# Norm weight applied at the gather, and each expert's gate, up and down matrices in one transfer

## The chip, the cores and the metric

The kernel runs on one core of one Trainium2 chip. The metric is the device time of the whole program in microseconds, lower is better: the median of several executions. A profile is one further execution, recorded by the hardware profiler.

## What is computed

A two-layer encoder trunk over 256 tokens of width 1024, all in float32. Cut to what matters here:

```
for l in range(2):
    h = rms_norm(x, norm_mix[l])
    x = x + concat[diff_attn, sparse_attn, latent_attn](h @ w_in[l]) @ w_out[l]
    n = rms_norm(x, norm_ffn[l])                  # norm_ffn: the weight that the change moves
    # router: 1 of 4 groups, then 2 of its 8 experts, for each token
    for e in range(32):
        h_e = silu(n[tokens of e] @ w_gate[l, e]) * (n[tokens of e] @ w_up[l, e])
        x[tokens of e] += gate_weight * (h_e @ w_down[l, e])
out = rms_norm(x, norm_final)
```

The weights `w_gate`, `w_up` (1024 x 512 each) and `w_down` (512 x 1024) of one expert are 6.29 MB together. 2 layers x 32 experts make 402.7 MB, and every expert is computed, for at most 32 tokens at a time.

## The kernel before

**Stages.** Each layer has an attention part (projections with `w_in` in six chunks, 16 attention steps, output projection with `w_out` in two halves), then the router, then the expert part: four rounds (`m`) of eight experts (`BODY`). Within a round the tokens are gathered twice, for four experts each (`QUAD`), by TensorE products with a selection matrix `pick`. The engines are programmed by hand, each with its own instruction list; semaphores order them.

**One expert on the engines.** TensorE multiplies the gathered tokens `xg` by gate and up (`gate_up`, L1751), transposes (L1762, L1765), multiplies by down (`down`, L1776), and adds the weighted rows into PSUM sums (`scatter`, L1786). ScalarE copies `gu_ps` out (`products_out`, L821 frees the gate/up place), takes the exponent (L806) and copies `y` (`y_out`, L832 frees the down place). VectorE makes the hidden values (`hidden`). TensorE runs `products(e)` first and `down_of(e - 1)` behind it, except for the last expert of a round, where `down_of` of the one before comes ahead of it.

**Where weights lie and what loads them.** SyncE (SP) issues nearly all transfers, in the order of its program, and waits for a semaphore ahead of an issue where the target is still in use. All of them go through one queue, q1. The gate/up matrices of expert `e` lie side by side in DRAM (`gate_up`, 32768 bytes in each of 128 partitions) and go to one of four places (`gu_place[e % 4]`: three pairs of slots of `ring`, and `late_place` in `arena`). The down matrix (`w_down`, 16384 bytes in each partition) goes to one of three places (`d_place[e % 3]`: slots 7 and 6 of `ring`, and `xb`). `ring` has eight slots of 16384 bytes per partition; `xb` behind it holds `x` and the attention bias. `loads_of(m)` gives the order of the issues of a round: gate/up of `e`, then down of `e - 1`. L563 issues gate/up, L573 down.

**Before the first expert.** `first_experts(l)` (L465 to L504) loads the first four experts while the attention part runs, each into slots as the `w_in` and `w_out` chunks there come free. Three quarters of expert 3's down matrix go to spare places (`spare`); its last quarter is loaded at L573 once expert 0's down matrix has been used. The 128-fold broadcast row of `norm_ffn` (`gain_ffn`) is loaded here too, at L480.

**The norm weight.** VectorE multiplies `x` by `gain_ffn` into `weighted` (`weight`, L1124); ScalarE scales the result by the row's `rms` and reorders it into `rows` (L642, called `copy`); the gathers read `rows`. The copies of a gather out of PSUM into `xg` are two of 128 x 512 (`gathered`, L642).

**The end of layer 0.** SP loads the chunks of `w_in` of layer 1 into the slots as the last experts are done with them, with nine small vectors (`load_small`, L441) behind the second chunk, then the bias and `w_out`.

**The start.** VectorE waits for `consts_in` at the head of its program, TensorE ahead of its second run of warm-up products (L1474).

## Time and profile before

| | us |
|---|---|
| median of 3 runs | 1176.25 (1175.04 to 1177.41) |
| the profiled execution | 1173.85 |
| its recorded span | 1171.9 |

| engine | busy, us | share of the span |
|---|---|---|
| TensorE, products | 930.9 | 79% |
| VectorE | 335.0 | 29% |
| ScalarE | 195.2 | 17% |
| DMA queue q1, 444.54 MB | | 90.3% of 16 engines |

The two expert parts run from about 158 us to 584 us and from about 738 us to the end. "DMA share" in the rows below is the share of a stretch in which the 16 DMA engines were moving packets; a little over 1 is an artefact of the edges. A packet is one contiguous run of bytes of one partition, so that a transfer into 128 partitions has 8 packets on each of the 16 DMA engines; packets "under 512 B" between long transfers are the notices of completion, 16 for each transfer.

### The profile page before, as it was taken

How to read it: one execution, taken by the hardware profiler on the slowest of the kernel's cores; microseconds unless marked ns; L12 is line 12 of the kernel's file. 1: busy time of each engine (PE TensorE's matmuls, PEld its weight loads, DVE VectorE, ACT ScalarE, POOL GpSimd, SP SyncE). 2: the span in 40 equal slices, each digit the busy share in tenths (PEclk: the TensorE clock that was granted, in tenths of full speed). 3: DMA queues.
4: the chain of work that ended last, by engine and by line, in shares of the span. 5: the costliest groups of instructions: out<-in, count | busy, mean ns of one | idle time of the engine just before them, and what ended most of it. 6: DMA issues, size and time to landing. Idle time of an engine off the chain costs nothing.

```text
span 1171.9 us, 23254 instructions
## 1 busy us (share of the span) xinstructions
PE 930.9 (79%) x10294; PEld 582.0 (50%) x10299; DVE 335.0 (29%) x978; ACT 195.2 (17%) x527; POOL 18.7 (2%) x38
## 2 busy tenths in 40 slices
PE   8999999767567766775899999997776677557765
PEld 5876666434334433543478766664343434234433
DVE  3656552211111111111137465521111111111112
ACT  2234321001000100110112442211010001001002
POOL 1000000000000000000010001000000000000000
PEclk9999999989888888888999999999887888788878
DMA  7956499999999999999998256999999999999995
GB/s 308 404 237 258 200 379 423 435 428 428 427 433 426 429 426 435 425 429 427 401 386 322 80 218 270 382 429 430 427 430 427 429 426 431 428 430 427 428 424 245
DMA packets 34455, 446.16 MB, mean 381 GB/s; under 512 B 9648, under 2 KB 11056, under 8 KB 14256
## 3 DMA queue, kind: packets, MB, share of 16 engines
q1 hardware_dynamic: 33792, 444.54, 90.3%
q8 instruction: 84, 1.38, 0.5%
q10 hardware_dynamic: 560, 0.09, 0.0%
q14 instruction: 19, 0.16, 0.0%
HBM read 443.57 MB, written 1.05 MB: 379 GB/s over the span
## 4 chain that ended last, share of the span: by engine, by line
DMA 50%; PE 45%; issue 2%; DVE 1%; ACT 1%; another core or an unknown queue 0%; SPq 0%; ACTq 0%; POOLq 0%; POOL 0%; DVEq 0%
DMA ring<-in_w_down 18%; DMA arena<-in_gate_up 14%; DMA xb<-in_w_down 14%; PE pv L1751 10%; PE pj L1374 8%; PE tr L1776 5%; DMA ring<-in_gate_up 3%; PE pj L1380 2%; PE tr L1735 2%; PE pj L1486 2%; PE pj L1786 2%; PE pj L1606 2%; PE pj L1581 1%; PE pj L1615 1%; PE lg L1404 1%
## 5 line engine op out<-in xcount | busy, mean ns | idle before, releaser
L1751 PE MATMUL pv<-ring,xT 128*32 128x256 f32 x3072 | 228.5, 458 | 110.8 <-DMA ring<-in_gate_up 110.8
L1751 PEld LDWEIGHTS pv<-ring,xT 128*32 128x32 f32 x3072 | 110.2, 127 | 218.0 <-DMA ring<-in_gate_up 109.8
L1222 DVE TENSOR_SCALAR arena<-arena 128x128 f32<-128x128 f32 x64 | 14.5, 227 | 667.2 <-ACT arena L806 666.9
L1751 PE MATMUL pv<-arena,xT 128*32 128x256 f32 x1024 | 85.5, 500 | 67.1 <-DMA arena<-in_gate_up 67.1
L642 ACT ACTIVATE arena<-pv 128x256 f32<-128x256 f32 x64 | 24.6, 384 | 513.3 <-PE pv L1751 513.3
L1374 PE MATMUL pj<-xT,ring 128*128 128x256 f32 x448 | 100.2, 381 | 0.0
L1776 PE MATMUL tr<-ring,arena 128*32 128x256 f32 x1360 | 81.9, 380 | 16.5 <-issue 10.1
L1751 PEld LDWEIGHTS pv<-arena,xT 128*32 128x32 f32 x1024 | 38.7, 139 | 112.6 <-DMA arena<-in_gate_up 73.4
L1374 PEld LDWEIGHTS pj<-xT,ring 128*128 128x128 f32 x448 | 84.3, 190 | 12.9 <-issue 1.1
L1786 PE MATMUL pj<-arena 32*128 32x256 f32 x512 | 72.5, 400 | 6.7 <-ACT arena L642 6.7
L1786 PE MATMUL lg<-arena 32*128 32x256 f32 x512 | 72.5, 401 | 0.0
L1776 PEld LDWEIGHTS tr<-ring,arena 128*32 128x32 f32 x1360 | 44.1, 109 | 48.6 <-issue 14.3
L642 ACT ACTIVATE arena<-tr 128x256 f32<-128x256 f32 (+3 forms) x106 | 41.2, 407 | 156.9 <-PE tr L1776 134.7
L1735 PE MATMUL tr<-arena,rows 128*128 128x128 f32 x448 | 58.6, 293 | 7.5 <-issue 7.5
L1735 PEld LDWEIGHTS tr<-arena,rows 128*128 128x128 f32 x448 | 55.7, 206 | 12.4 <-issue 12.4
L1223 DVE RECIPROCAL arena<-arena 128x128 f32<-128x128 f32 x64 | 61.0, 953 | 2.2
L1786 PEld LDWEIGHTS pj<-arena 32*128 32x128 f32 x512 | 44.5, 184 | 23.1 <-issue 22.0
L1776 PE MATMUL tr<-xb,arena 128*32 128x256 f32 x640 | 38.4, 380 | 8.5 <-DMA xb<-in_w_down 4.7
L1786 PEld LDWEIGHTS lg<-arena 32*128 32x128 f32 x512 | 43.8, 184 | 0.0
L1765 PE MATMUL pv<-con,arena 128*32 128x128 f32 x1024 | 41.2, 279 | 0.0
L1762 PE MATMUL pv<-con,arena 128*128 128x128 f32 x128 | 32.4, 335 | 9.5 <-ACT arena L642 9.5
L1762 PEld LDWEIGHTS pv<-con,arena 128*128 128x128 f32 x128 | 20.2, 207 | 37.3 <-issue 19.7
(237 smaller groups left out, 856.8 us busy)
## 6 DMA issues: line engine op xcount, KB each, us to landing
ring<-in_gate_up SPq DMA_DIRECT2D x42, 4096.0 KB, 48.5
ring<-in_w_down SPq DMA_DIRECT2D x38, 2048.0 KB, 41.4
arena<-in_gate_up SPq DMA_DIRECT2D x14, 4096.0 KB, 41.9
xb<-in_w_down SPq DMA_DIRECT2D x18, 2048.0 KB, 40.8
ring<-in_w_in_chunks SPq DMA_DIRECT2D x10, 2048.0 KB, 21.3
ring<-in_gate_up SPq DMA_DIRECT2D x10, 2048.0 KB, 8.2
ring<-in_w_out_halves SPq DMA_DIRECT2D x4, 2048.0 KB, 33.2
arena<-in_gate_up SPq DMA_DIRECT2D x4, 2048.0 KB, 49.4
```

Of the source, the lines that this page charges most:

```text
L642: return nc.scalar.activation(out, in_, ACT.Copy, **k)
L1223: own.link(v.reciprocal(e_neg, e_neg))
L1374: ins = mm(out, w[:, j], xT[:, j, :], start=(j == 0), stop=(j == KD - 1))
L1380: ins = mm(out, src[:, j, t * P:(t + 1) * P], weights(i, n)[:, j, c:c + m], start=(j == 0), stop=(j == KD - 1))
L1486: ins = mm(bank[:, 0:R5], xT_raw[:, j, t * P:(t + 1) * P], weights(0, n5)[:, j, :], start=(j == 0), stop=(j == KD - 1))
L1606: mm(pj[:, half], mixT_up[:, t, k - KD // 2, :], chunk(6 + half, 512)[:, k, :], start=(k == KD // 2), stop=False)
L1735: ins = mm(wide_ps[:, j * n:(j + 1) * n], rows[:, t, j * P:(j + 1) * P], pick[:, t, 0:n], start=(t == 0), stop=(t == TOK - 1))
L1751: ins = mm(gu_ps[i * CAP:(i + 1) * CAP, :], xg[:, j, c:c + CAP], w, start=(j == 0), stop=(j == KD - 1), tile_position=(0, i * CAP), skip_g ...
L1762: turn_(h_ps[:, c].rearrange("p h s -> p (h s)"), by_step[:, c], ident)
L1765: ins = mm(pgt_ps[k * CAP:(k + 1) * CAP, t * P:(t + 1) * P], pgate[:, t, i, :], ident, start=True, stop=True, tile_position=(0, k * CAP), ...
L1776: ins = mm(tr[i * CAP:(i + 1) * CAP, 0, 0:SEQ], hid[:, b, k % 2, k // 2, :], rows_of[k][:, SEQ * i:SEQ * (i + 1)], start=(k == 0), stop=(k ...
L1786: ins = mm(sums[i][:, SEQ * t:SEQ * (t + 1)], pgT[r, b, t, :], y[r, :], start=False, stop=last, tile_position=(i * CAP, 0), skip_group_che ...
```

## The change

**Layout.** In DRAM one array `experts` holds gate, up and down of an expert side by side, 49152 bytes in each partition. In SBUF `ring` and `xb` become one tensor `ring_xb`; its first nine slots are three places of three slots each (`whole`). A place takes all of one expert. `late_place` is a fourth place, for the gate/up matrices of expert 3 and of expert 31 (`LATE`, `LAST`); the down matrices of those two go to four spare pieces. Experts 4 to 30 go round the three places.

**Transfers.** Expert 0, and experts 6 to 28, come in one transfer each, which waits for the place's gate/up and down to be both used. Expert 1, 2, 4, 5, 29, 30 still come in parts. The down matrix of expert 31 comes in four pieces instead of three.

**Norm weight.** `gain_ffn`, its transfer and the VectorE products are gone. ScalarE copies `x` with the scale `rms` into `rows`, and each gather is copied to `xg` in eight pieces of 128 x 128, each with the weight of its 128 columns as scale (`gain_G`, one value per partition); TensorE waits piece by piece.

**Waits.** `consts_in` is waited for later, at the first use of the identity. `load_small` of layer 1 stands behind the third chunk of `w_in` and waits for expert 31's down matrix to be used, since one of its targets is a spare piece.

```diff
+PLACES, LATE = 3, 3
+AHEAD = PLACES + 1
+LAST = N_EXPERTS - 1
+def place(e):
+    return e if e < AHEAD else LATE if e == LAST else (e - AHEAD) % PLACES
 def loads_of(m):
-    order = [("gu", 0)]
-    for e in range(1, BODY - 1):
-        order += [("gu", e), ("d", e - 1)]
-    late = [("gu", BODY - 1), ("d", BODY - 2)] if m == ROUNDS - 1 else [("d", BODY - 2), ("gu", BODY - 1)]
-    return [(kind, m * BODY + e) for kind, e in order + late + [("d", BODY - 1)]]
+    first, last = max(m * BODY, AHEAD), (m + 1) * BODY
+    if m == 0:
+        order = [("d", AHEAD), ("gu", AHEAD + 1), ("d", AHEAD + 1)]
+        return order + [("all", e) for e in range(AHEAD + 2, last)]
+    if m < ROUNDS - 1:
+        return [("all", e) for e in range(first, last)]
+    order = [("gu", LAST - 2), ("gu", LAST - 1), ("d", LAST - 2), ("gu", LAST), ("d", LAST - 1), ("d", LAST)]
+    return [("all", e) for e in range(first, LAST - 2)] + order
...
+        whole = [ring_xb[:, 3 * i * SLOT:3 * (i + 1) * SLOT] for i in range(PLACES)]
+        gu_place = [flat.rearrange("p (j n) -> p j n", j=KD) for flat in [w[:, 0:2 * SLOT] for w in whole] + [late_place]]
+        d_place = [w[:, 2 * SLOT:].rearrange("p (k n) -> p k n", k=KE) for w in whole]
...
                 sp.wait_ge(win_used[1], l + 1)
-                sp.dma_start(gu_place[0], gu[0]).then_inc(gu_full[0], 16)
                 sp.wait_ge(win_used[2], l + 1)
+                sp.dma_start(whole[0], experts_d[l * N_EXPERTS]).then_inc(gu_full[0], 16)
...
-                sp.dma_start(gain_ffn, bcast_row(norm_ffn, l, D_MODEL)).then_inc(gain_f_in, 16)
+                sp.dma_start(spare[3], down[LATE][:, 3]).then_inc(spare_full[3], 16)
...
+                        i, n = place(e), l * N_EXPERTS + e
+                        if kind != "d":
+                            sp.wait_ge(gu_used[i], at(l, FILLS[i], uses(i, e)))
+                        if kind != "gu":
+                            sp.wait_ge(d_used[i], at(l, FILLS[i], uses(i, e)))
+                        if kind == "all":
+                            sp.dma_start(whole[i], experts_d[n]).then_inc(gu_full[i], 16)
...
-                    act.wait_ge(x_weighted, at(l, TOK, t + 1))
+                    act.wait_ge(x_added, at(l, PARTS, (2, PARTS)[t]))
...
-                        for half in range(2):
-                            act.wait_ge(wide_done, at(r, WIDE, gather_use(q) + half))
-                            copy(xg[:, 4 * half:4 * half + 4, :].rearrange("p j s -> p (j s)"), tr[:, half]).then_inc(wide_read, 1)
+                        for j in range(KD):
+                            if j % 4 == 0:
+                                act.wait_ge(wide_done, at(r, WIDE, gather_use(q) + j // 4))
+                            copy(xg[:, j, :], wide_ps[:, j * P:(j + 1) * P], scale=gain_G[:, l, j:j + 1]).then_inc(wide_read, 1)
...
-                weight(0, 0, D_MODEL).then_inc(x_weighted, 1)
...
-                own.mark(weight(1, 512, D_MODEL))
...
-                weight(1, 0, 512).then_inc(x_weighted, 1)
```

On SyncE's queue, in the first round of layer 0, behind the load of the rest of expert 4's gate/up: `in_gate_up` 128x8192 is gate and up of an expert, `in_w_down` 128x4096 its down matrix, `in_experts` 128x12288 all three. The waits name the semaphores of the places (`gu_used`, `d_used`). Before:

```order
L503 DMA ring<-in_gate_up 128x4096 [waits gu_used0]
L573 DMA ring<-in_w_down 128x1024 [waits d_used0]
L563 DMA ring<-in_gate_up 128x8192 [waits gu_used1]
L573 DMA ring<-in_w_down 128x4096 [waits d_used1]
L563 DMA ring<-in_gate_up 128x8192 [waits gu_used2]
L573 DMA xb<-in_w_down 128x4096 [waits d_used2]
L573 DMA ring<-in_w_down 128x4096 [waits d_used0]
L563 DMA arena<-in_gate_up 128x8192 [waits gu_used3]
```

And now:

```order
L504 DMA ring_xb<-in_experts 128x4096 [waits gu_used0]
L577 DMA ring_xb<-in_experts 128x4096 [waits d_used0]
L572 DMA ring_xb<-in_experts 128x8192 [waits gu_used1]
L577 DMA ring_xb<-in_experts 128x4096 [waits d_used1]
L567 DMA ring_xb<-in_experts 128x12288 [waits d_used2,gu_used2]
L567 DMA ring_xb<-in_experts 128x12288 [waits d_used0,gu_used0]
```

The quarter of expert 3's down matrix (128x1024) has left this place, and from expert 6 on one issue with two waits stands for two issues with one each; the load of expert 7 now waits for the place of expert 4 rather than for that of expert 3.

On SyncE's queue at the end of layer 0, from the last gate/up matrix to the first small vector of layer 1. Before:

```order
L561 DMA arena<-in_gate_up 128x4096
L573 DMA ring<-in_w_down 128x4096 [waits d_used0]
L570 DMA ring<-in_w_down 128x2048 [waits d_used1]
L570 DMA ring<-in_w_down 128x1024 x2
L517 DMA ring<-in_w_in_chunks 128x3520 [waits gu_used0]
L517 DMA ring<-in_w_in_chunks 128x4096 [waits gu_used0]
L441 DMA lowrank<-in_mla_q_norm 128x256
```

And now:

```order
L570 DMA arena<-in_experts 128x4096
L577 DMA ring_xb<-in_experts 128x4096 [waits d_used2]
L575 DMA xT<-in_experts 128x1024 [waits d_used3]
L575 DMA arena<-in_experts 128x1024
L575 DMA lowrank<-in_experts 128x1024
L575 DMA arena<-in_experts 128x1024
L520 DMA ring_xb<-in_w_in_chunks 128x3520 [waits gu_used0]
L520 DMA ring_xb<-in_w_in_chunks 128x4096 [waits gu_used0]
L520 DMA ring_xb<-in_w_in_chunks 128x4096 [waits d_used0]
L443 DMA lowrank<-in_mla_q_norm 128x256 [waits d_used3]
```

The third chunk of `w_in` now stands ahead of the small vectors, and these wait for `d_used3`, the use of expert 31's down matrix.

## Rows read from the trace of the kernel before

**Rows 1.** windows of the trace (busy time of each engine, PEclk, DMA share, GB/s)

```profile
60.00:132.00 72.00, 71.54 (x354) 47.59 (x353) 40.99 (x116) 29.00 (x99) 1.02 (x1) 1.00 0.53 205
132.00:160.00 28.00, 27.54 (x182) 20.87 (x185) 17.25 (x68) 11.64 (x22) 3.34 (x3) 1.00 0.92 374
...
250.00:540.00 290.00, 199.10 (x2696) 116.71 (x2696) 45.92 (x115) 26.66 (x70) 0.00 (x0) 0.85 1.00 429
830.00:1130.00 300.00, 208.31 (x2826) 121.32 (x2826) 46.37 (x117) 27.61 (x73) 0.00 (x0) 0.84 1.00 428
```

**Rows 2.** the chain of waits in order of time

```profile
252.86 41.62 DMA xb<-in_w_down
```

**Rows 3.** the transfer of the norm weight (first and last start, us)

```profile
L480 SPq DMA_DIRECT2D arena<-in_norm_ffn x2: 431/431/431, 102.9 to 682.9; - x2
```

**Rows 4.** DMA queues, 250 to 350 us (packets, MB, share of 16 engines)

```profile
DMA packets 1975, 42.87 MB, mean 429 GB/s; under 512 B 215, under 2 KB 215, under 8 KB 215
...
q1 hardware_dynamic: 1968, 42.76, 99.9%
```

**Rows 5.** the same, 33 to 40 us

```profile
q1 hardware_dynamic: 203, 2.98, 99.5%
```

**Rows 6.** the same, 558 to 565 us

```profile
q1 hardware_dynamic: 205, 2.98, 100.5%
```

**Rows 7.** timeline of TensorE, one expert of round 2, layer 0

```profile
304.48 5.80 PE L1751 MATMUL pv<-ring,xT 128*32 128x256 f32 x64 [5.93 <-DMA ring<-in_gate_up]
310.11 1.90 PE L1776 MATMUL tr<-ring,arena 128*32 128x256 f32 x32
```

**Rows 8.** timeline of SyncE's queue, the same stretch

```profile
312.12 0.33 SPq L573 DMA_DIRECT2D ring<-in_w_down  x1
```

**Rows 9.** line L482, a transfer of 2048 KB with nothing ahead of it

```profile
DMA to landing us min/median/max: 7.3/7.4/7.4
```

**Rows 10.** chain of waits, round 4 of layer 1

```profile
1036.61 6.67 PE pv L1751 x63
...
1062.05 4.31 PE pv L1751 x63
```

**Rows 11.** line L503, the last part of expert 4's gate/up

```profile
DMA to landing us min/median/max: 9.9/10.3/10.7
```

**Rows 12.** timeline of SyncE's queue, after expert 4

```profile
203.14 0.33 SPq L573 DMA_DIRECT2D ring<-in_w_down  x1
```

**Rows 13.** timeline of all engines, 0 to 20 us

```profile
6.07 1.29 DVE L911 TENSOR_TENSOR rows<-arena,gain_T 128x512 f32<-128x512 f32 x2 [5.15 <-remote]
6.82 9.13 PE L1486 MATMUL pj<-ring,rows 128*128 128x440 f32 x24
...
15.00 0.35 DVE L915 TENSOR_SCALAR arena<-con,rms 128x128 f32<-128x128 f32 x1 [0.90 <-POOL rms L606]
...
15.78 0.61 PE L1469 MATMUL lg<-arena,con 128*128 128x128 f32 x4
```

**Rows 14.** timeline, 128 to 175 us: rms of the last token tile and the router

```profile
151.48 0.84 POOL L606 TENSOR_TENSOR rms<-ssq,con 128x1 f32<-128x1 f32 x1 [13.84 <-DVE ssq L1129]
...
152.38 0.26 DVE L1137 SCALAR_TENSOR_TENSOR arena<-pv,rms,br 128x40 f32<-128x40 f32 x1 [0.47 <-POOL rms L606]
```

**Rows 15.** a copy of 128x128 by ScalarE

```profile
204.11 0.28 ACT L806 ACTIVATE arena<-pv 128x128 f32<-128x128 f32 x1 [0.54 <-PE pv L1765]
```

**Rows 16.** timeline of TensorE, the end of layer 0

```profile
576.72 1.93 PE L1776 MATMUL tr<-ring,arena 128*32 128x256 f32 x32 [1.21 <-DMA ring<-in_w_down]
...
581.76 0.16 PEld L1776 LDWEIGHTS tr<-ring,arena 128*32 128x32 f32 x8 [0.33 <-DMA ring<-in_w_down]
```

**Rows 17.** timeline of SyncE's queue, the start of layer 1

```profile
588.45 1.88 SPq L517 DMA_DIRECT2D ring<-in_w_in_chunks  x4
```

**Rows 18.** timeline of VectorE, the start of layer 1

```profile
602.71 1.41 DVE L949 SCALAR_TENSOR_TENSOR arena<-arena,rms,lowrank 128x256 f32<-128x256 f32 x4 [0.42 <-POOL rms L606]
...
611.88 0.35 DVE L976 SCALAR_TENSOR_TENSOR arena<-arena,xb 128x128 f32<-128x128 f32 x1 [6.91 <-ACT arena L733]
```

More of the change, by code:

```diff
@@ L169, in upto @@
     def upto(last):
-        return sum(D_LOADS.get(n, 1) for n in range(last) if n < N_EXPERTS - 1 and n % D_PLACES == e % D_PLACES)
+        return sum(D_LOADS.get(n, 0) for n in range(last) if place(n) == place(e))
     return 16 * at(layer, upto(N_EXPERTS), upto(e + 1))
@@ L575, in _ @@
-            sp.wait_ge(gu_used[GU_PLACES - 1], DEPTH * GU_FILLS)
+                        i, n = place(e), l * N_EXPERTS + e
[5 more added lines that the diff above has]
+                            sp.dma_start(whole[i], experts_d[n]).then_inc(gu_full[i], 16)
+                        elif kind == "gu" and e == LAST:
+                            for part, (a, b) in enumerate(LAST_STEPS):
+                                sp.dma_start(gu_place[i][:, a:b], gu_v[n][:, a:b]).then_inc(last_steps_in[part], 16)
+                        elif kind == "gu":
+                            sp.dma_start(gu_place[i], gu_v[n]).then_inc(gu_full[i], 16)
+                        elif e == LAST:
+                            for k in range(KE):
+                                sp.dma_start(spare[k], down_v[n][:, k]).then_inc(last_in[k], 16)
+                        else:
+                            sp.dma_start(d_place[i], down_v[n]).then_inc(d_full[i], 16)
@@ L1771, in down @@
                     for k in range(KE):
[L1772 to L1774 removed]
+                        if in_pieces:
+                            pe.wait_ge(last_in[k], 16 * (l + 1))
                         for i in range(4):
```

215 lines of the change are left out of this document (95 added, 120 removed).

## Prediction

> **What bounds the kernel now.** I read the page's slices first, then the windows by stage, then the DMA queues, and the engines' timelines last. The page gives TensorE 79% busy and q1 90.3%, and both are averages over two kinds of stage. The windows separate them [rows 1]. From 60 to 132 us TensorE is busy 71.5 of 72 us and the DMA share is 0.53: the attention part hangs on TensorE, and transfers have room. From 250 to 540 us, and from 830 to 1130 us in layer 1, TensorE is busy only 199.1 of 290 and 208.3 of 300 us, at a granted clock of 0.85, while the DMA share is 1.00 at 428 to 429 GB/s. From 132 to 160 us the share is already 0.92. So each expert part is one stream of bytes that starts near 132 us of its layer and is full from about 160 us on; its end comes at (bytes of the stream) / (rate), whatever the other engines do, as long as each load is issued in time. One expert is 6.29 MB, 14.66 us at 429 GB/s. The chain of waits names SyncE's waits for places too (a load 41.62 us between issue and landing [rows 2]), but 41.6 us is nearly three experts of queue: such a wait is no loss while the queue is full. I therefore price the change by what it takes out of the stream, what it makes each byte cost, what it moves at the stream's start, and whether a load can now be late.
>
> **Bytes taken out.** The broadcast row of the norm weight (0.52 MB) is loaded at 102.9 and 682.9 us, in the stretch with room [rows 1, 3]. Its transfer goes, and the last quarter of expert 3's down matrix, 0.52 MB, takes its place there; that quarter leaves the full stream. 0.524 / 429 = 1.22 us for each layer, **-2.44 us** in all. This is sure as far as the stream is full, which rows 1 say.
>
> **Fewer and longer packets.** A transfer of 16384-byte rows, alone in the queue, shows what a packet costs: from 33 to 40 us q1 moves 2.98 MB (182 packets of 16384 bytes) in 99.5% of 16 x 7 us, 612 ns each [rows 5]; from 558 to 565 us the same 2.98 MB in 100.5%, 618 ns each [rows 6]. From 250 to 350 us q1 moves 42.76 MB in 1968 packets, of which 215 are notices; the other 1753 are 16384 or 32768 bytes, and the bytes say 896 and 857 of them [rows 4]. They take 99.9% of 1600 us, so a 32768-byte packet takes (1598.4 - 896 x 612) / 857 = 1225 ns, or 1219 ns by the other value. Twice 612 less 1225 is -1 ns, twice 618 less 1219 is 17 ns: a packet costs between nothing and 17 ns beyond its bytes. I take the middle, 9 ns, since nothing singles out an end. A whole expert saves 8 packets and one notice on each engine, 9 x 9 = 81 ns. Of the whole experts 6 to 28 lie in the full stream, 23 for each layer (expert 0 has room): 46 x 0.081 = **-3.7 us**, with ends at 0 and 46 x 9 x 17 ns = -7.0 us. Expert 31's down matrix has one piece more and 8 rows more for each engine, +0.08 us at each layer's end, **+0.2**.
>
> The Trainium skill ("DMA: Bandwidth & Descriptors", section "Anatomy of one DMA") gives a DMA about 2.0 us of fixed cost beside its bytes. By that alone, 46 transfers fewer would be worth 92 us. The trace speaks against it here: a stream with two transfers in each 14.66 us runs at a DMA share of 1.00 [rows 1], so the fixed part of one lies beside the bytes of another. The same page puts the ceiling at 435 GB/s ("Where 436 GB/s comes from"); an estimate by that page is that no packet size could give more than 1.4% of the stream.
>
> **Can a load be late?** Before, up to three experts were queued; now the load for expert e + 3 waits until both parts of expert e are used. In the trace the first product of an expert starts at 304.48, its 32 products and the down product of the expert before it end near 312, and SyncE issues at 312.12: 7.6 us after the landing [rows 7, 8]. A transfer of 2.10 MB with nothing ahead lands 7.4 us after its issue [rows 9], 2.5 us more than its bytes take. The next load is thus ready 10.1 us after a landing where 14.66 are allowed: 4.5 us to spare. The worst place is the fourth round, where TensorE reads the overflow count: products that follow expert 23's at 1036.61 start at 1062.05, 25.4 us later [rows 10]. Expert 25 would land 29.3 us after expert 23, the products of 24 end at 25.4 + 4.3 = 29.7, so only half a us is lost there and the margin stays above 2. In steady state I book nothing.
>
> The one tight place is at the stream's start, where TensorE still runs ahead. The rest of expert 4's gate/up is issued at 162.0 and lands 10.3 us later, at 172.3 [rows 11]. Behind it now come expert 4's down, all of 5 and all of 6: 14.68 MB, 34.2 us, so expert 6 lands near 206.5. Expert 7 must go to expert 4's place, whose down matrix is used at 203.14 [rows 12]; issued then, it lands at 203.14 + 2.5 + 14.66 = 220.3, against 221.2 for an unbroken stream. A margin of 0.9 us; TensorE's extra waits in the gathers can eat it. I book **+0.3 us** for each layer, ends 0 and 1.5, **+0.6** in all.
>
> **The norm weight.** VectorE loses three multiplies. The one on the way to the last gather stands while GpSimd takes 0.84 us for the rms, and the router's first step idles 0.47 us until that rms is there [rows 14]; TensorE's last router product ends at about the same moment, so I book 0, at best -0.3 for each layer. ScalarE's copies become eight of 128 columns. One such copy takes 0.28 us [rows 15], a little more with a scale; a gate/up step (one eighth of 3.8 to 5.8 us [rows 7]) lasts 0.47 us or more, so the copies stay ahead of TensorE. 0; if that cover were gone, 8 x 0.28 - 1.2 = 1.0 us at the two gathers of a first round, the others lie in TensorE's idle time.
>
> **The start.** VectorE's first multiply starts at 6.07 us after the wait for `consts_in`, TensorE's first product 0.75 us later [rows 13]. Without that wait the product can start about 0.5 us earlier; the next gate is VectorE's second diagonal, ready at 15.35, against TensorE at 15.78 [rows 13]: **-0.4 us**, which shifts everything behind it. Ends 0 and -0.5.
>
> **Between the layers.** The small vectors now wait for expert 31's down product, near 582 us [rows 16]. Ahead of them in the queue are three chunks, 5.9 MB or 13.7 us after the last expert, so they land near 600 us. VectorE needs them at 602.71, and after them it idles 6.91 us before 611.88 [rows 18]: 9 us of cover, 0. The third chunk was issued at 588.45 with three others [rows 17]; it is earlier now, the others within a few us.
>
> **Sum.** -2.4 - 3.7 + 0.2 + 0.6 - 0.4 = -5.7 us. The profiled execution takes 1173.85 us (span 1171.9 and 2 us around it), so 1168.1 by the sum; the median of the runs is 2.4 us above it, 1176.25 - 5.7 = **1170.5**.
>
> **Rivals.** (1) The rows are cut again, or a packet's time is all bytes: the packet term is 0 and the time 1174.2, within 0.2%. For it: the lower end of the estimate from rows 4 to 6 is zero. Against it: 16384- and 32768-byte rows both show as one packet each, and the two windows' mean is above zero. 0.14. (2) Late loads make it slower. The place: the issue behind `y_out`. The mechanism is that it must come within 14.66 - 2.5 = 12.2 us of a landing, against 7.6 now. If the queue needs more than one transfer of lead, because some of the 16 engines run ahead, each us missed costs 1 us on every transfer; confined to the 14 experts behind a gather at 1 us each it gives +14 - 5.7, 1184.5; on all 46, 1216. It decides where the lead falls below 2.5 us plus the engines' spread. Against it: margins of 4.5 and above 2 us. 0.07. (3) The same late issue only at the stream's start, at its full 1.5 us in each layer: +2.4, 1172.9, inside the forecast's range. (4) The fixed-cost rule: faster by tens of us, 1084; at a DMA share of 1.00 there is nothing to win it from. 0.01.
>
> **How the numbers follow.** The forecast with its unknowns (packets 0 to -7.0, start of the stream 0 to 3, rms 0 to -0.6) spans about 1166 to 1174 and has 0.78. Below it lies little; above it, rival 1 at 1174.2 belongs in the range and rival 2 does not. Range **1166.0 to 1174.8**. Faster than 1173.9 (0.2% is 2.35 us, about what a measurement of this kernel can tell from no change): 0.77 + 0.01 and a part of rival 1's spread, 0.80. Same: 0.13. Slower: 0.07.
>
> **What would show it.** The DMA share in the stretch of whole experts stays at 1.00 and the rate rises from 429 to 431 or 432 GB/s; packets of 49152 bytes take less than one of each kind before. If the rate stays at 429, the packet term was wrong; if the share falls below 1, loads are late, and the idle time stands behind `y_out` on SyncE. TensorE's first product starts near 6.3 us, layer 0's last down product 3.5 us earlier than now. What would make it wrong: a lower rate for the 49152-byte pitch, or a gap around expert 7 of more than 1.5 us.

## The result and the profile after the change

| | before | after |
|---|---|---|
| median of the runs | 1175.04 us (1174.32 to 1177.41) | 1168.97 us (1167.60 to 1169.34) |
| profiled execution, span | 1171.9 us | 1166.2 us |
| ratio after / before, 95% interval | | 0.9945, 0.9932 to 0.9958 |

The change makes the kernel 6.1 us faster between the medians; the interval goes from 4.9 to 8.0 us. The forecast was 5.7 us faster, 1170.5 us in a range of 1166.0 to 1174.8. (It counted from 1176.25, the median of three runs; over five runs the kernel before has 1175.04.) A second set of five runs of the changed kernel gave 1169.05 us beside 1174.65.

The windows of the changed kernel (busy time of each engine, granted clock, DMA share, GB/s) answer to [rows 1]:

```profile
60.00:132.00 72.00, 71.53 (x353) 47.37 (x352) 40.83 (x116) 29.02 (x99) 1.02 (x1) 1.00 0.52 205
132.00:160.00 28.00, 27.26 (x182) 20.72 (x184) 14.55 (x63) 12.55 (x28) 2.12 (x3) 1.00 0.93 375
...
250.00:540.00 290.00, 200.92 (x2760) 117.61 (x2760) 44.48 (x112) 32.36 (x100) 0.00 (x0) 0.85 1.00 429
830.00:1130.00 300.00, 209.08 (x2890) 122.45 (x2890) 47.90 (x120) 33.42 (x103) 0.00 (x0) 0.85 1.00 429
```

They look like those of before, and that is what the reader has to see first: the expert parts are still one full stream, and the rate that a window prints (whole GB/s) is too coarse for a change of half a percent. The prediction's own sign ("If the rate stays at 429, the packet term was wrong"), read from these lines, would have struck out a term that was right. A finer ruler is needed. The products of an expert start when its load has landed, so in a stretch where TensorE waits for every expert their starts are the landings of the stream. The timeline of TensorE in layer 0 of the changed kernel (start, duration, and in brackets the idle time and what ended it):

```profile
282.09 5.65 PE L1746 MATMUL pv<-ring_xb,xT 128*32 128x256 f32 x64 [4.90 <-DMA ring_xb<-in_experts]
296.63 3.89 PE L1746 MATMUL pv<-ring_xb,xT 128*32 128x256 f32 x64 [1.31 <-DMA ring_xb<-in_experts]
311.17 6.43 PE L1746 MATMUL pv<-ring_xb,xT 128*32 128x256 f32 x64 [6.84 <-DMA ring_xb<-in_experts]
```

Twice 14.54 us. The kernel before, whose products at 304.48 stand in [rows 7], has the next ones at

```profile
319.10 5.41 PE L1751 MATMUL pv<-ring,xT 128*32 128x256 f32 x64 [5.01 <-DMA ring<-in_gate_up]
```

so 14.62 us. Some steps of both kernels are longer (15.0 us, say), but these are the quiet ones, and they are 0.08 us apart. In bytes that is 6.29 MB in 14.62 us and in 14.54 us, 430.3 and 432.7 GB/s: the rate did rise, as the prediction said.

The end of layer 0 in the changed kernel, TensorE again: the second half of expert 31's gate/up, expert 30's down product, and the last quarter of expert 31's.

```profile
567.80 2.02 PE L1746 MATMUL pv<-arena,xT 128*32 128x256 f32 x32 [2.05 <-DMA arena<-in_experts]
572.75 3.59 PE L1770 MATMUL tr<-ring_xb,arena 128*32 128x256 f32 x32 [1.25 <-DMA ring_xb<-in_experts]
...
579.43 0.61 PE L1770 MATMUL tr<-arena 128*32 128x256 f32 x8
```

Before, the same three stood at 571.82, 576.72 and 581.76 ([rows 16] has the last two; 581.76 is the weight load that opens the last quarter). The stream arrives 4.0 us earlier, the layer ends only 2.4 us earlier (layer 1's first product starts at 584.61, before at 586.98). Between them stands expert 30's down product: 3.59 us for 32 products that took 1.93 us before [rows 16]. The window of 570 to 575 us says why, PEclk is 0.77:

```profile
570.00:575.00 5.00, 3.33 (x42) 1.80 (x46) 2.09 (x5) 0.64 (x2) 0.00 (x0) 0.77 1.04 426
```

For part of that window TensorE ran at the lower of its two levels (1.2 instead of 2.4 GHz), after idle times of 2.05 and 1.25 us between short pieces of work. No term of the forecast spoke of that. In layer 1 the same product took 1.93 us in this execution.

### The profile page after: what moved, and what is told of

It is laid out like the page before. It is cut to its first block, busy times and chain, and to the rows that moved or that the text cites. A ratio compares the mean times of both kernels' runs of the same rounds, so it can differ in the third digit from the quotient of the medians.

```text
span 1166.2 us, 23346 instructions
## 1 busy us (share of the span) xinstructions
PE 920.8 (79%) x10299; PEld 578.4 (50%) x10299; DVE 329.8 (28%) x972; ACT 212.6 (18%) x623; POOL 16.3 (1%) x38
## 4 chain that ended last, share of the span: by engine, by line
DMA 49%; PE 47%; issue 1%; DVE 1%; ACT 1%; POOL 0%; ACTq 0%; POOLq 0%; SPq 0%; DVEq 0%
DMA ring_xb<-in_experts 49%; PE pv L1746 13%; PE pj L1371 8%; PE tr L1770 6%; PE pj L1377 2%; PE pj L1481 2%; PE pj L1601 2%; PE pj L1780 2%; PE pj L1576 1%; PE pj L1610 1%; PE lg L1401 1%; PE pv L1760 1%; PE tr L1411 1%; PE tr L1677 1%; PE tr L1730 1%
## 5 line engine op out<-in xcount | busy, mean ns | idle before, releaser
L1746 PE MATMUL pv<-ring_xb,xT 128*32 128x256 f32 x3840 | 286.2, 459 | 181.7 <-DMA ring_xb<-in_experts 181.7
L1746 PEld LDWEIGHTS pv<-ring_xb,xT 128*32 128x32 f32 x3840 | 135.7, 127 | 320.7 <-DMA ring_xb<-in_experts 197.5
L1770 PE MATMUL tr<-ring_xb,arena 128*32 128x256 f32 x1920 | 116.7, 383 | 19.8 <-issue 15.2
L1371 PE MATMUL pj<-xT,ring_xb 128*128 128x256 f32 x448 | 100.2, 381 | 0.0
L1770 PEld LDWEIGHTS tr<-ring_xb,arena 128*32 128x32 f32 x1920 | 64.2, 110 | 63.7 <-issue 21.6
L1371 PEld LDWEIGHTS pj<-xT,ring_xb 128*128 128x128 f32 x448 | 84.1, 190 | 13.1 <-issue 1.1
L646 ACT ACTIVATE xT<-tr,gains 128x128 f32<-128x128 f32 x128 | 36.4, 370 | 66.8 <-PE tr L1730 66.7
L646 ACT ACTIVATE arena<-pj 64x256 f32<-64x256 f32 (+2 forms) x48 | 21.0, 442 | 71.0 <-PE pj L1371 52.4
L699 ACT ACTIVATE arena<-arena,nmax 128x128 f32<-128x128 f32 (+1 forms) x64 | 28.6, 447 | 25.2 <-DVE nmax L1046 24.8
```

Of the source, the lines that this page charges most:

```text
L646: return nc.scalar.activation(out, in_, ACT.Copy, **k)
L699: ins = nc.scalar.activation(prob[:, s % 2, m * nk(t):(m + 1) * nk(t)], logit[:, s % 2, m * nk(t):(m + 1) * nk(t)], ACT.Exp, bias=nmax[:, ...
L1371: ins = mm(out, w[:, j], xT[:, j, :], start=(j == 0), stop=(j == KD - 1))
L1746: ins = mm(gu_ps[i * CAP:(i + 1) * CAP, :], xg[:, j, c:c + CAP], w, start=(j == 0), stop=(j == KD - 1), tile_position=(0, i * CAP), skip_g ...
L1770: ins = mm(tr[i * CAP:(i + 1) * CAP, 0, 0:SEQ], hid[:, b, k % 2, k // 2, :], rows_of[k][:, SEQ * i:SEQ * (i + 1)], start=(k == 0), stop=(k ...
```

## The experiments

All kernels but the first are the changed kernel as it is or with one edit (two edits where the name has two parts), timed against the kernel before (1174.4 to 1175.0 us, by the set). Two more, with delayed loads, follow at the end of this section. The table has, beside the time, three numbers from the timelines: when the second half of expert 31's gate/up starts (the end of the stream as TensorE sees it), and what expert 30's down product took, in layer 0 and layer 1.

| kernel | median us | ratio (95%) | expert 31, layer 0 / 1 | down 30, us |
|---|---|---|---|---|
| before | 1174.7 | 1 | 571.82 / 1151.12 | 1.93 / 1.94 |
| changed, first | 1168.97 | 0.9945 (0.9932 to 0.9958) | 567.80 / 1145.35 | 3.59 / 1.93 |
| changed, again | 1169.05 | 0.9953 (0.9940 to 0.9966) | 567.81 / 1145.82 | 3.31 / 1.93 |
| two pieces | 1170.38 | 0.9965 (0.9952 to 0.9978) | 569.78 / 1147.62 | 1.93 / 1.93 |
| six pieces | 1183.92 | 1.0085 (1.0072 to 1.0098) | 576.64 / 1160.61 | 1.93 / 1.93 |
| quarter in the stream | 1170.58 | 0.9969 (0.9959 to 0.9980) | 568.60 / 1144.86 | 1.93 / 1.93 |
| expert 7 in two | 1168.24 | 0.9949 (0.9936 to 0.9963) | 567.58 / 1145.09 | 3.48 / 3.39 |
| first wait back | 1168.55 | 0.9958 (0.9944 to 0.9971) | 567.94 / 1143.21 | 1.93 / 3.62 |
| zeros at the end | 1167.36 | 0.9942 (0.9929 to 0.9956) | 568.09 / 1143.23 | 1.93 / 1.93 |
| zeros and expert 7 in two | 1167.21 | 0.9936 (0.9922 to 0.9949) | 568.22 / 1144.55 | 1.93 / 1.93 |
| two pieces, zeros | 1170.59 | 0.9960 (0.9945 to 0.9974) | 569.78 / 1147.21 | 1.93 / 1.93 |
| quarter, zeros | 1169.78 | 0.9951 (0.9935 to 0.9966) | 570.10 / 1147.30 | 1.93 / 1.93 |

An interval is about 1.5 us to each side, so two rows of the table that are 1 us apart are not told apart by their times. Rows of different sets carry the drift of the kernel before too, up to 0.6 us. The columns from the timelines are of one profiled execution each. In two places, the quarter with zeros in layer 0 and the zeros in layer 1, the product follows right behind the products of zeros, so the landing was a little earlier than the number.

One more number from the same executions ties the columns to the time. From the start of expert 31's second half in layer 1 to the end of the profiled execution it is 22.7 to 22.8 us in nine of the twelve rows, six pieces and the kernel before among them. It is 24.2 and 24.3 us in the two whose down product of layer 1 took 3.39 and 3.62 us. In the quarter's, 24.75 us, the last piece of expert 31's down matrix landed late:

```profile
1156.31 0.64 PE L1770 MATMUL tr<-arena 128*32 128x256 f32 x8 [1.37 <-DMA arena<-in_experts]
```

So the time is the end of the stream, and the clock or a late last piece on top of it.

**The changed kernel again.**

> The changed kernel once more, beside the experiments of the same call. Both theories: 5 to 7 us under the kernel before (the first measurement gave 6.1 between the medians), 1168 to 1170 us. It is the base line for the three kernels that follow.

1169.05 us, as expected. Expert 31 started at 567.81 us in layer 0, and expert 30's down product ran at the lower clock there too (3.31 us).

**The price of a packet.** Each of the 46 whole loads as two transfers, then as six:

```
-  sp.dma_start(whole[i], experts_d[n]).then_inc(gu_full[i], 16)
+  sp.dma_start(gu_place[i], gu_v[n]).then_inc(gu_full[i], 16)
+  sp.dma_start(d_place[i], down_v[n]).then_inc(gu_full[i], 16)
```

> The changed kernel with each of the 46 whole loads issued as two transfers again, rows of 32768 and of 16384 bytes, to the same places, behind the same waits, and used only when both have landed. Nothing moves but the number of packets. Theory (a packet costs some 9 ns beside its bytes, and a transfer one notice on each of the 16 engines): 8 packets and one notice more for each engine and expert, 81 ns, so 3.7 us slower than the changed kernel, about 1172. Rival (the packets cost nothing, and the gain is in the bytes, the start or the order of the first loads): no difference, 1168 to 1169.

> The same with six transfers of 8192 byte rows for each of the 46 loads, so that the price of a packet shows several times over. Theory: 40 packets and 5 notices more for each engine and expert at 9 ns, 0.405 us, times 46 = 18.6 us slower than the changed kernel, about 1187; at the upper end of the estimate from the trace of before, 17 ns, 33 us. Rival (a packet's time is its bytes alone): no difference. The DMA share stays at 1.00 in both; the rate tells them apart, 417 GB/s against 430.

Two pieces: 1170.38 us, 1.3 us above the changed kernel, between theory and rival. Six pieces: 1183.92 us, 14.9 us above, where 18.6 and 0 were the bets; the rival is dead. The quiet steps on TensorE's timeline say it without the scatter of whole runs. Two pieces, then six pieces:

```profile
297.40 3.83 PE L1748 MATMUL pv<-ring_xb,xT 128*32 128x256 f32 x64 [1.16 <-DMA ring_xb<-in_experts]
312.01 6.57 PE L1748 MATMUL pv<-ring_xb,xT 128*32 128x256 f32 x64 [6.97 <-DMA ring_xb<-in_experts]
```

```profile
284.63 5.25 PE L1750 MATMUL pv<-ring_xb,xT 128*32 128x256 f32 x64 [5.22 <-DMA ring_xb<-in_experts]
299.53 3.83 PE L1750 MATMUL pv<-ring_xb,xT 128*32 128x256 f32 x64 [2.07 <-DMA ring_xb<-in_experts]
314.42 5.69 PE L1750 MATMUL pv<-ring_xb,xT 128*32 128x256 f32 x64 [7.25 <-DMA ring_xb<-in_experts]
```

14.61 us in two pieces, 14.90 and 14.89 in six, 14.54 in one. Against one piece, two have 9 packets and notices more on each engine, six have 45 more: 0.07 / 9 = 7.8 ns and 0.355 / 45 = 7.9 ns. One price fits both.

The steps alone can't say that it is the packet that costs: in both kernels a transfer more is nine packets and notices more, and 71 ns for each transfer fits them as well. The kept traces do, since they have every packet's own time. In the full stream the medians are 312 ns for 8192 bytes, 612 for 16384, 1214 for 32768, 1815 for 49152 and 9 for a notice. Each 16384 bytes more are 601 to 602 ns, so every packet has about 11 ns beside its bytes, whatever its size. The packets' times add up to 1.01 of the window in six pieces and to 1.00 in one, so they overlap a little, and 7.9 ns is what the stream pays.

The queue of the six pieces from 250 to 350 us shows the same without TensorE:

```profile
q1 hardware_dynamic: 5747, 41.88, 100.8%
```

41.88 MB where the changed kernel moved 43.11 MB in 985 packets in the same 100 us. A window of 100 us cuts rows of 49152 bytes at its ends, so this one is only good for the sign.

**Why two pieces cost only 1.3 us.** Their stream ended 2.0 us later in layer 0 (569.78 against 567.80), but their down product ran at the full clock and the changed kernel's did not. So the same two kernels were compared with the clock held up, by products of zeros in waits that are there anyway:

```
   if in_pieces and j == first:
+      if n == 1:
+          keep_warm(5)
       pe.wait_ge(last_steps_in[n], 16 * (l + 1))
...
   turned(BODY - 1)
+  keep_warm(4)
   down_of(BODY - 2)
```

> The changed kernel with nine products of zeros added at the end of each layer: five between the halves of expert 31's gate/up, four ahead of expert 30's down product, all in time in which TensorE waits for a transfer (gaps of 1.2 to 2.05 us, a product of zeros takes 0.23). They add zeros to a sum. Theory: at the end of layer 0 the granted clock falls to the lower level (0.77 from 570 to 575 us), expert 30's down product takes 3.59 us there where it takes 1.93 in layer 1 and took 1.93 before, and this keeps 1.66 us of the gain: with the engine busy it takes 1.93, and the whole is 1.5 us faster than the changed kernel, about 1167.4. Rival (that product is hidden behind expert 31's down matrix, which lands at 578.7): no difference, or slower by what the zeros take.

> The 46 whole loads in two transfers each, as in the earlier run, and the nine products of zeros in the waits at a layer's end, as in the other. That run was only 1.3 us slower than the changed kernel, but its last expert came 2.0 us (layer 0) and 2.3 us (layer 1) later, and its down product there ran at the full clock where the changed kernel's ran at the lower one. Theory (the lower clock hid the price of the packets): with the clock held up in both, the two pieces cost 46 x 0.073 us = 3.4 us against the kernel with the zeros alone (1167.4), 1170 to 1171. Rival (the packets are worth 1.3 us and the rest is scatter): 1168.7.

The zeros alone: 1167.36 us, 1.6 us under the changed kernel's 1169.0, as bet. The end of layer 0:

```profile
571.72 1.04 PE L1716 MATMUL pj<-zeros 128*128 128x512 bf16 x4
572.98 1.93 PE L1772 MATMUL tr<-ring_xb,arena 128*32 128x256 f32 x32 [0.22 <-DMA ring_xb<-in_experts]
...
578.10 0.64 PE L1772 MATMUL tr<-arena 128*32 128x256 f32 x8
```

Expert 30's down matrix landed 0.2 us later than in the changed kernel (572.98 against 572.75), its product took 1.93 us and the layer's last product starts 1.3 us earlier (578.10 against 579.43). The same window has PEclk 1.00:

```profile
570.00:575.00 5.00, 4.11 (x58) 1.94 (x54) 2.10 (x5) 0.66 (x2) 0.00 (x0) 1.00 1.02 419
```

Two pieces with the zeros: 1170.59 us, 3.2 us above the zeros alone, with 3.4 expected. The two were timed in different sets; beside their own kernels of before the difference is 2.8 us. No run of one is as fast as the slowest of the other (1169.77 and up against 1168.42 and down). The packets are worth about 3.3 us of this kernel by the quiet steps, and the lower clock hid about half of it in the first comparison. Of the seven profiled executions in the table with the new order and without the zeros, four had this product at the lower clock in one layer or in both; of the four with the zeros, none. The times show a gain of the zeros of 1.6 us for the changed kernel, and 0.8 and -0.2 us for the quarter and the two pieces, whose down products were at the full clock in their profiled execution without them. A single one of these differences is at the edge of the scatter. The timelines are plainer: layer 1's first product starts at 584.2 to 584.6 us in the three kernels whose down product of layer 0 was slow, and at 583.2 to 583.5 us in the three (first wait back, and the two with zeros) where it was not and the stream was the same.

**The bytes.** Expert 3's last quarter goes back behind expert 3's gate/up, and its new place stays empty:

```
-  sp.wait_ge(lg_done, at(l, NS, 8))
-  sp.dma_start(spare[3], down[LATE][:, 3]).then_inc(spare_full[3], 16)
...
   sp.dma_start(gu_place[LATE], gu[LATE]).then_inc(gu_full[LATE], 16)
+  sp.wait_ge(lg_done, at(l, NS, 8))
+  sp.dma_start(spare[3], down[LATE][:, 3]).then_inc(spare_full[3], 16)
```

> The changed kernel with the last quarter of expert 3's down matrix (0.52 MB) loaded behind expert 3's gate/up again, in the full stream, where it stood before, and nothing in its new place. This takes back what the norm weight's row made room for. Theory: 1.22 us for each layer at 429 GB/s, 2.4 us slower than the changed kernel, about 1171; the landing of every later load comes 1.2 us later. Rival (the stream's start has idle time that takes it up, since loads there wait for places): under 1 us.

> The quarter of expert 3's down matrix in the full stream, as in the earlier run, and the nine products of zeros. Theory (expert 7's load is set by TensorE's use of expert 4, so of the 1.22 us in each layer only about half is gained): 1.2 us slower than the kernel with the zeros alone, about 1168.6. Rival (the bytes count in full, 2.44 us, and the earlier 1.5 us had the clock's scatter in it): 1169.8.

1.5 us slower without the zeros, 2.4 us with them (2.0 beside their own kernels of before). That is nearer to the full 2.44 us than to the 1.2 of the second run's theory, but with intervals of 1.5 us neither is ruled out.

The edit is not quite the kernel before: here the quarter is loaded from 144 to 146 us, where it was issued at 168.99 before, behind the last part of expert 4's gate/up. That place was dearer than its bytes. The last part of expert 4's gate/up, issued at 161.98, landed 10.7 us later (the longest of [rows 11]), at 172.7. The quarter behind it (line L573, issued at 168.99):

```profile
DMA to landing us min/median/max: 7.1/7.1/7.1
```

It landed at 176.1, 3.4 us after the load ahead of it, where its bytes take 1.22 us; in layer 1 it was 3.25 us by the landings kept in the trace. Its 128 packets of 4096 bytes took 280 ns each on average, 281 in layer 1, where such packets take 159 ns at the layers' other places, such as 109 to 118 us, and 162 to 164 at the layers' ends. (Only the program's first transfer has 237.) On each engine that is 8 x 0.12 = 1.0 us above the price of the bytes, in each layer. In the changed kernel the quarter is loaded ahead of the full stream, where its packets take 159 ns, and in these two runs they take 170 to 178 ns. No run put the quarter back at its old place, and why its packets were slow there is not known.

What the start of the stream shows is small: with the quarter behind expert 3's gate/up, the products of experts 6 and 7 start at

```profile
209.42 5.32 PE L1746 MATMUL pv<-ring_xb,xT 128*32 128x256 f32 x64 [3.56 <-DMA ring_xb<-in_experts]
223.95 3.83 PE L1746 MATMUL pv<-ring_xb,xT 128*32 128x256 f32 x64 [2.19 <-DMA ring_xb<-in_experts]
```

a quiet step of 14.53 us. In the changed kernel they are 14.94 us apart, and there the load of expert 7 comes a little late:

```profile
207.62 5.37 PE L1746 MATMUL pv<-ring_xb,xT 128*32 128x256 f32 x64 [2.44 <-DMA ring_xb<-in_experts]
222.56 3.84 PE L1746 MATMUL pv<-ring_xb,xT 128*32 128x256 f32 x64 [2.55 <-DMA ring_xb<-in_experts]
```

**The late load of expert 7.** Its gate/up is issued behind the products of expert 4, its down matrix behind expert 4's down product:

```
-  return order + [("all", e) for e in range(AHEAD + 2, last)]
+  order += [("all", AHEAD + 2), ("gu", AHEAD + 3), ("d", AHEAD + 3)]
+  return order + [("all", e) for e in range(AHEAD + 4, last)]
```

> The changed kernel with expert 7's load issued as gate/up (behind the products of expert 4 alone) and down (behind expert 4's down product), so that the queue has work while TensorE finishes expert 4. In the changed kernel the DMA share is 0.94 from 205 to 210 us of layer 0, where it was 1.04 before. Theory (the late load of expert 7 costs the slowest engine 0.4 us in each layer: expert 7 lands 14.94 us after expert 6, a quiet expert 14.53): the whole is 0.5 to 0.8 us faster than the changed kernel, less 0.15 for one packet more in each row; the share there is 1.0 again. Rival (the slowest of the 16 engines still has work when the load comes late, so only the others idle): the share returns to 1.0 and the time stays, within 0.2 us.

> The changed kernel with both small changes: products of zeros in TensorE's waits at the end of a layer, and expert 7's load in two. Theory: the first is worth 1.2 to 1.7 us (a down product at the lower clock in one of the two layers), the second nothing that can be measured (0.3 us by the first try, while the slowest engine had work left), so 1167 to 1168 us, at least as fast as any so far. Rival (they add up): 1166.5.

The window of 205 to 210 us, in the changed kernel and then with the load in two:

```profile
205.00:210.00 5.00, 2.56 (x28) 1.16 (x28) 1.62 (x4) 0.00 (x0) 0.00 (x0) 0.75 0.94 364
```

```profile
205.00:210.00 5.00, 2.73 (x32) 1.18 (x28) 1.67 (x4) 0.00 (x0) 0.00 (x0) 0.75 0.99 423
```

The hole in the share closes. The time hardly answers: 1168.24 against 1169.0 without the zeros, 1167.21 against 1167.36 with them, both inside the scatter. The timelines say why. Expert 7's products start anywhere from 222.56 to 224.07 us in the four profiled executions that have the same loads up to there (changed first and again, first wait back, zeros), but expert 12's start at 296.63 to 296.91 in all four, and at 296.30 and 296.79 with the load in two. What the late load costs at expert 7 is made up by expert 12, within 0.3 us. That is the rival of the first run (only the faster engines idle), and the second run's bet (nothing that can be measured) held.

**The start.** TensorE waits for the constants ahead of its first product again:

```
+  if l == 0:
+      pe.wait_ge(consts_in, 16)
   def turn_in(t):
```

> The changed kernel with TensorE's wait for the constants put back ahead of its first product. Theory of the prediction: 0.4 us slower, TensorE's first product at 6.8 us and not at 6.47. What the two traces suggest instead: the first product comes 0.35 us later, and the first expert's products start at 158.0 us all the same, as they do in both kernels (157.98 and 158.02), so no difference in the time.

1168.55 us, no difference. The profiled execution did not show the later first product either: it is at 6.53 us with the wait back, and at 6.24 to 6.79 us in the twelve profiled executions of the new order without it. So the 0.35 us between the two first traces is no larger than what executions of one program differ by, and this run can't test it. What the traces do show is where such a gain would end. TensorE's first product in the changed kernel, and the first products of expert 0:

```profile
6.47 9.02 PE L1481 MATMUL pj<-ring_xb,rows 128*128 128x440 f32 x24
...
158.02 3.83 PE L1746 MATMUL pv<-ring_xb,xT 128*32 128x256 f32 x64
```

Before, they stood at 6.82 [rows 13] and 157.98. TensorE is 0.30 us ahead up to its products at 147.81 us (148.11 before); then VectorE adds their result at

```profile
150.28 0.42 DVE L1127 TENSOR_TENSOR ring_xb<-tr,ring_xb 128x256 f32<-128x256 f32 x1 [2.01 <-PE tr L1631]
```

which is 0.50 us behind the end of those products; before it was 0.15 us. All thirteen profiled executions of the new order have this 0.50 us, whatever their start, and their first expert starts at 157.89 to 158.72 us. Why VectorE starts that much later is open.

**How much lead a load has.** GpSimd delays each whole load by four or by ten small operations (the code is shortened):

```
   rms_of(own, base, 7, 15, 16)
+  for n, e in enumerate(WHOLE):
+      pool.wait_ge(d_used[place(e)], at(l, FILLS[place(e)], uses(place(e), e)))
+      for _ in range(4):                                   # 10 in the second
+          own.link(tensor_tensor(idle, idle, con[C_HALF], ALU.pow))
+      pool.sem_inc(delayed, 1)
...
+  sp.wait_ge(delayed, at(l, len(WHOLE), WHOLE.index(e) + 1))
   sp.dma_start(whole[i], experts_d[n]).then_inc(gu_full[i], 16)
```

> The changed kernel with a delay ahead of each of the 46 whole loads: GpSimd waits for the place, does four small linked operations of about 0.6 us each (2.5 us), and only then lets SyncE issue. Theory (4.5 us of lead to spare in the steady state): the margin takes it up, time as the changed kernel, 1168 to 1170, although faster engines may run dry, so that the mean DMA share falls below 1.00. Rival (the lead has to cover the spread of the 16 engines too, 4 to 5 us between the first and the last of a transfer): 2.5 + 4.5 - 4.5 = 2.5 us late for every second load, some 50 us slower.

> The delay ahead of each of the 46 whole loads made longer: ten linked operations of GpSimd and not four, 6 us where it was 2.4. The short delay cost 11.9 us over the changed kernel, so the margin is used up at about 2.4 us in places and not yet everywhere. Theory (a load must be issued 12.2 us after the landing of the one before it, it is issued 7.6 after; what is late beyond that is lost once for every two loads): 6 - 4.6 = 1.4 us over two loads, 32 us, and with the 0.5 us for each load that the short delay cost beside it, 30 to 45 us slower than the changed kernel, 1200 to 1213. Rival (all of the added 3.6 us is lost on every load, since the lead is gone already): 1180.5 + 46 x 3.6 = 1346; half of that, if it is lost once for every two loads: 1263.

The short delay: 1180.51 us (ratio 1.0050, 1.0034 to 1.0066), 11.5 us slower than the changed kernel, neither nothing nor 50. The long one: 1229.18 us (1.0469, 1.0444 to 1.0494), 60 us slower, beyond the 30 to 45 of the theory and far from 178. The timeline of the long delay in round 2 of layer 0 (GpSimd's rows are the delay itself, SyncE issues 0.15 us behind their end; the products start when their load has landed):

```profile
290.77 5.50 PE L1757 MATMUL pv<-ring_xb,xT 128*32 128x256 f32 x64 [8.25 <-DMA ring_xb<-in_experts]
298.16 6.26 POOL L641 TENSOR_TENSOR idle<-idle,con 128x1 f32<-128x1 f32 x10 [11.30 <-ACTq L849]
305.55 3.83 PE L1757 MATMUL pv<-ring_xb,xT 128*32 128x256 f32 x64 [1.71 <-DMA ring_xb<-in_experts]
...
322.55 6.62 PE L1757 MATMUL pv<-ring_xb,xT 128*32 128x256 f32 x64 [9.36 <-DMA ring_xb<-in_experts]
...
331.05 6.27 POOL L641 TENSOR_TENSOR idle<-idle,con 128x1 f32<-128x1 f32 x10 [13.51 <-ACTq L849]
...
356.36 5.15 PE L1757 MATMUL pv<-ring_xb,xT 128*32 128x256 f32 x64 [5.52 <-DMA ring_xb<-in_experts]
```

Counted from the end of the delay, the load issued at 304.4 lands at 322.55, 18.1 us later and 17.0 us after the one before it; the load issued at 337.3 lands at 356.36, 19.0 us later. Its bytes take 14.54 us, so a whole load needs a lead of 3.6 to 4.5 us, not 2.5, and has to be issued within 10.0 to 10.9 us of a landing. The changed kernel issues about 7.6 us after it, as before [rows 7, 8]: a margin of 2.4 to 3.3 us. The changed kernel itself has one load at this limit: expert 7's, issued at 203.2 when 4.4 us were left to the landing before it, lands 19.3 us later and 0.4 us late. The short delay sits just at the same edge:

```profile
284.24 6.48 PE L1757 MATMUL pv<-ring_xb,xT 128*32 128x256 f32 x64 [6.21 <-DMA ring_xb<-in_experts]
292.60 2.50 POOL L641 TENSOR_TENSOR idle<-idle,con 128x1 f32<-128x1 f32 x4 [14.00 <-ACTq L849]
299.59 3.83 PE L1757 MATMUL pv<-ring_xb,xT 128*32 128x256 f32 x64 [1.29 <-DMA ring_xb<-in_experts]
...
314.12 5.27 PE L1757 MATMUL pv<-ring_xb,xT 128*32 128x256 f32 x64 [6.88 <-DMA ring_xb<-in_experts]
```

Issued at 295.1, 10.9 us after the landing at 284.24, this load still lands a quiet 14.53 us behind its forerunner, while others of this run come 0.8 to 2 us late. The rival's claim that the spread of the engines needs lead of its own was half right: the lead is 1 to 2 us longer than a lone transfer says, not 4.5.

The Trainium skill gives about 2.0 us of fixed cost for a transfer ("DMA: Bandwidth & Descriptors", section "Anatomy of one DMA") and puts most of it into the confirmation that the last byte has landed. The section is on transfers that GpSimd issues; these are issued by SyncE, so it bears on them, and on the prediction's fourth rival, only as a rough guide. Here the runs show that a fixed part is lead and not time of the stream: six pieces have 230 transfers more than one and cost 14.9 us, 65 ns each, where 2.0 us each would be 460 us.

## Why the prediction was right, point by point

- **The bound** was read rightly: in both kernels and the variants of the table the time follows the end of the stream, to 0.1 us where the clock stays up and the last piece is not late.
- **Packets: -3.7 us booked, 3.2 measured** (two pieces against one, clock held up), 3.3 by the quiet steps (46 x 0.071). Of the range of 0 to 17 ns the prediction took the middle, 9 ns, and said that nothing singled it out; it measured 7.9 ns. That it came so near is luck in part, the sign and the mechanism are not. The range of 0 to 17 ns came from windows whose edges cut packets; the starts of products gave the number in two lines, and could have been read from the kernel before for its own step.
- **Bytes: -2.44 us booked, 2.4 and 1.5 measured** by the two pairs, for a quarter that stands earlier than before. At its old place it took about 1.0 us more in each layer than its bytes, by its packets' times: some 4.4 us in all. The step that was off is "0.524 / 429 = 1.22 us for each layer", which took the rate of long packets for a transfer of 4096-byte ones without looking at its landing.
- **Late load at the stream's start: +0.6 us booked** for both layers, nothing found. The place was right, and the step from expert 6 to 7 is 0.4 us too long in layer 0 (up to 2.3 in the other executions), but by expert 12 it is made up within 0.3 us, and closing the hole gave 0.15 to 0.8 us, which the times can't tell from nothing. The prediction took a late landing at one expert for a loss of the stream.
- **Steady state: nothing booked, nothing lost**, but with less to spare than written, 2.4 to 3.3 us and not 4.5. The step that was off is the lead, taken as 2.5 us from a transfer alone in the queue [rows 9]; it is 3.6 to 4.5 us.
- **Norm weight: nothing**, as booked. ScalarE's eight copies end in time (expert 0's products start 0.04 us later than before), and VectorE's first router step starts at 152.43 us, 152.38 before [rows 14], although three multiplies are gone. No run moved the norm weight by itself, so this rests on the timelines.
- **The start: -0.4 us booked, nothing found.** The step that failed is "which shifts everything behind it". The first expert is not earlier: VectorE's 0.35 us more at 150 us would take up such a gain. Whether the first product is earlier at all is not shown, since executions differ by as much. The prediction had followed the gain to 15.78 us and not to the end of the attention part.
- **Between the layers: nothing**, as booked: VectorE takes the small vectors at 600.35 us, 15.7 us after TensorE's first product of layer 1 at 584.61, and before at 602.71 [rows 18], 15.7 us after 586.98.
- **The end of a layer: missed.** The prediction said that layer 0's last down product would come 3.5 us earlier. The stream came 4.0 us earlier and TensorE gave back 1.66 us, because expert 30's down product ran at the lower clock. It happened in one of two layers in this execution, and in 5 of the 14 layers of the seven without zeros. The sum has no term for it.
- **The stream gave more than booked:** 4.0 us in layer 0 and 3.4 in layer 1 (5.77 less the 2.37 by which layer 1 starts earlier; 2.6 to 4.2 in the other executions with whole loads), 7.4 against 5.5 us. Two pieces with the zeros, which has the packet sizes of before for these loads, is 4.1 to 4.3 us faster than the kernel before (3.1 to 6.5 by the interval), of which the bytes at 429 GB/s explain 2.4. The timelines place the other 1.7 to 1.9 us ahead of expert 12 in each layer. From expert 12 to 28 the two kernels take the same time, first before, then two pieces with the zeros:

```profile
289.72 3.90 PE L1751 MATMUL pv<-ring,xT 128*32 128x256 f32 x64 [1.86 <-DMA ring<-in_gate_up]
...
526.73 3.83 PE L1751 MATMUL pv<-ring,xT 128*32 128x256 f32 x64 [1.00 <-DMA ring<-in_gate_up]
```

```profile
297.32 3.83 PE L1750 MATMUL pv<-ring_xb,xT 128*32 128x256 f32 x64 [1.28 <-DMA ring_xb<-in_experts]
...
534.13 3.83 PE L1750 MATMUL pv<-ring_xb,xT 128*32 128x256 f32 x64 [1.88 <-DMA ring_xb<-in_experts]
```

That is 237.01 and 236.81 us. At expert 12 the new order has 4.19 MB more behind it (two down matrices, 9.7 us), so it stands 2.1 us further: 1.2 for the quarter's bytes and 0.9 beyond them. The 1.0 us by which the quarter's packets were slow at their old place is of this size, in both layers. With it the two terms of the stream come to 3.3 + 4.4 = 7.7 us, against the 7.4 that it gave. No run tests it; the new places of the loads are a rival that the traces do not exclude.
- **Luck in the total.** The total agrees to 0.4 us in part because unbooked losses (the clock, the start) and this unbooked gain cancel.

The fastest kernel measured is the changed one with the zeros and expert 7's load in two, 1167.21 us (0.9936 of before), 1.8 us under the changed kernel; the zeros alone have the same within 0.2 us.

## What to carry to other kernels

Where a stream of transfers is full, price a change of its shape by packets and bytes, and measure the price where the consumer waits for each transfer: the differences of its starts resolve a few hundredths of a microsecond, windows and whole runs do not. Price the slack of a ring at its worst place, behind a gather or a count, and by a run that delays the loads on purpose. Look at the landing of every small transfer inside a full stream: its bytes may be the smaller part of its price. When an engine that waits for the stream is at the end of the chain, look at its granted clock there: an earlier arrival can meet a slower engine.

## What the runs showed of the hardware

- On a full queue, packets of 8192 to 49152 bytes with their notices cost about 7.9 ns each beside the bytes (0.355 us for 45, 0.07 us for 9). Their own times have 11 ns beside the bytes (312, 612, 1214 and 1815 ns for 8192, 16384, 32768 and 49152 bytes).
- 128 packets of 4096 bytes took 280 ns each on average at one place in the full stream of the kernel before, in both layers, and 159 to 164 ns at all other places but the program's start.
- TensorE's clock fell to the lower level after two idle times of 2.05 and 1.25 us (PEclk 0.77 from 570 to 575 us), in 5 of 14 layers and not in the others, which had such idle times too (1.23 and 1.25 us ahead of the same product at the full clock); nine products of zeros (2.3 us of work in waits) kept it up in all eight layers of the four profiled kernels that had them. The Trainium skill ("TensorE: Matmul & The Clock Gate", section "HAM oscillation — how this bites in real kernels") describes short runs of products with waits for transfers between them as what lets the clock fall. The rows at 572.75 and 572.98 agree with that pattern, but the waits of the page's example are some 3 to 5 us long, and those of this case are shorter.
- A load of 6.29 MB issued as the queue ran dry landed 18.1 and 19.0 us after its issue, 3.6 and 4.5 us beyond its bytes, where a transfer of 2.10 MB alone showed 2.5 us.
